# A transformer stack on one core: each background weight-sum transfer gets a panel of its own, and lent slots join the ring at its end

## The reference

```
h = concat(meta, x)                                             # 528 x 1024
h = LN(a1 * h + even_mixer(h));   h = LN(a1 * h + relu(h @ w1)^2 @ w2)   # layer 0, d_ff 4096
h = LN(a1 * h + retention(h));    h = LN(a1 * h + relu(h @ w1)^2 @ w2)   # layer 1
h = h[16:]                                                      # 512 x 1024
h = LN(a2 * h + 0.5 * swiglu1(h));  h = LN(a2 * h + token_mixers(h))     # d_ff 2816
h = LN(a2 * h + cross_attention(h, mem));  out = LN(a2 * h + 0.5 * swiglu2(h))
```

## Time and profile before

| | |
|---|---|
| time, median of 3 runs | 2704.35 us (2703.06 to 2708.93) |
| profiled execution | 2705.15 us, span 2703.2 us, mean granted PE clock 0.992 |
| PE, PEld busy | 2633.5 us, 2347.4 us |
| DVE, ACT, POOL busy | 1455.0, 1120.3, 345.0 us |
| DMA moved | 342.61 MB, of it 79.70 MB by POOL's queue |
| stretches of the span | even mixer to about 305 us, layer 0 chunks 0 to 3 about 335, 421, 510, 598 to 680, retention to 1115, layer 1 chunks from 1185, 1252, 1337, 1422 to 1500, SwiGLU 1 to 1880, mixers to 2165, cross attention to 2300, SwiGLU 2 to the end |

### The profile page before, as it was taken

One profiled execution on the slowest core, in us unless ns is written; L12 is line 12 of the kernel. 1 busy time (PEld: TensorE's weight loads), 2 busy tenths in 40 slices (PEclk: granted clock), 3 DMA queues, 4 the chain that ended last, 5 costly groups with the idle time before them and its releaser, 6 DMA issues.

```text
span 2703.2 us, 41070 instructions
## 1 busy us (share of the span) xinstructions
PE 2633.5 (97%) x16968; PEld 2347.4 (87%) x16968; DVE 1455.0 (54%) x2464; ACT 1120.3 (41%) x1833; POOL 345.0 (13%) x414
## 2 busy tenths in 40 slices
PE   8999999999999999999999999999899999999997
PEld 6888999999988888888888988888888897989997
DVE  5664666446543434575556633334666764654655
ACT  4555444334433233353334432322557543433443
POOL 3100310001311000230000410011311130300002
PEclk9999999999999999999999999999999999999998
DMA  9911275335462512256344382252622132233542
GB/s 340 228 51 48 79 285 158 121 114 160 109 149 64 140 63 84 87 188 220 121 142 157 94 238 91 89 147 66 170 86 71 61 104 65 67 105 130 168 141 67
DMA packets 108840, 342.61 MB, mean 127 GB/s; under 512 B 11248, under 2 KB 13680, under 8 KB 108272
## 3 DMA queue, kind: packets, MB, share of 16 engines
q1 hardware_dynamic: 78448, 260.30, 29.3%
q0 software_dynamic: 30208, 79.70, 12.2%
HBM read 337.83 MB, written 81.79 MB: 155 GB/s over the span
## 4 chain that ended last, share of the span: by engine, by line
PE 86%; DVE 4%; ACT 3%; POOL 2%; issue 2%; DMA 2%; SPq 0%; DVEq 0%; POOLq 0%; ACTq 0%
PE ps L693 61%; PE ps L735 14%; PE ps L1040 2%; POOL R L3077 1%; PE ps L1171 1%; PE ps L743 1%; DMA RAW<-in_wf 1%; PE ps L935 1%; PE ps L895 1%; POOL S L3062 1%; PE ps L1026 1%; ACT HT L1445 1%; DVE HT L2186 1%; DVE R L2193 1%; DMA SCR<-in_wfb 1%
## 5 line engine op out<-in xcount | busy, mean ns | idle before, releaser
L2159 DVE TENSOR_TENSOR WL<-RAW,WH 128x1024 fp32r<-128x1024 f32 (+2 forms) x280 | 338.6, 1210 | 249.9 <-ACT WH L1401 248.5
L693 PE MATMUL ps<-HH,LENT 128*128 128x256 f32 (+2 forms) x1848 | 416.1, 321 | 8.8 <-DVE LENT L2159 8.8
L693 PE MATMUL ps<-XH,WH 128*128 128x264 f32 (+2 forms) x1360 | 412.1, 340 | 12.0 <-DVE XL L3036 7.4
L1401 ACT ACTIVATE WH<-RAW 128x1024 fp32r<-128x1024 f32 (+2 forms) x280 | 287.8, 1032 | 279.8 <-PE ps L693 181.8
L693 PE MATMUL ps<-XL,WH 128*128 128x264 f32 (+2 forms) x1360 | 398.7, 331 | 0.0
L693 PE MATMUL ps<-XH,WL 128*128 128x264 f32 (+2 forms) x1360 | 398.0, 330 | 0.0
L2159 DVE TENSOR_TENSOR LENT<-RAW,LENT 128x1024 fp32r<-128x1024 f32 (+2 forms) x220 | 261.2, 1193 | 181.9 <-ACT LENT L1401 180.2
L693 PE MATMUL ps<-XH,LENT 128*128 128x264 f32 (+2 forms) x1392 | 332.6, 328 | 5.3 <-DVE XL L2210 5.1
L693 PEld LDWEIGHTS ps<-HH,LENT 128*128 128x128 f32 x1848 | 302.9, 190 | 36.2 <-DVE LENT L2159 9.9
L1401 ACT ACTIVATE LENT<-RAW 128x1024 fp32r<-128x1024 f32 (+2 forms) x220 | 216.6, 994 | 276.0 <-PE ps L693 169.0
L693 PE MATMUL ps<-HH,WH 128*128 128x512 f32 (+2 forms) x928 | 285.6, 333 | 10.8 <-DVE HL L2252 6.7
(11 more groups left out here) (266 smaller groups left out, 4022.9 us busy)
## 6 DMA issues: line engine op xcount, KB each, us to landing
RAW<-in_wf SPq DMA_DIRECT2D x104, 512.0 KB, 4.3
sum_wf<-in_wf POOLq DMA_DIRECT2D x36, 1024.0 KB, 30.9
RAW<-sum_wf SPq DMA_DIRECT2D x48, 512.0 KB, 3.8
RAW<-in_wr SPq DMA_DIRECT2D x48, 512.0 KB, 3.5
RAW<-in_wg SPq DMA_DIRECT2D x37, 512.0 KB, 3.5
RAW<-in_wu SPq DMA_DIRECT2D x37, 512.0 KB, 4.1
RAW<-in_wd SPq DMA_DIRECT2D x32, 512.0 KB, 3.5
RAW<-in_we SPq DMA_DIRECT2D x24, 512.0 KB, 6.8
```

What stands on the lines that cost most here:

```text
L693: mm = e.matmul(o[:, to:to + m], wt, xt[:, k, c0 + a * m:c0 + (a + 1) * m], start=(n == 0 and j == 0), stop=(n == nk - 1 and j == 2))
L1401: e.activation(slot(u)[0][:, 0:n], raw[:, 0:n], ACT.Copy).then_inc(*S.w_hi(u))
L2159: e.tensor_tensor(lo[:, 0:n], raw[:, 0:n], hi[:, 0:n].bitcast(F32), ALU.subtract).then_inc(*S.w_lo(u))
```

## The change

Two edits. In `slot_plan` the slots of the three panels in `again` are put at the right end of the ring; all other slots that join are put at the left, as before. On POOL the copies and additions are issued one by one, each behind a wait for a panel that PE has finished: the 24 of layer 0 behind plan panels 3 to 26 of the even mixer, the 24 of layer 1 behind the `wf2` panels of chunks 0 to 2 of layer 0, the 16 of the SwiGLU behind those of chunks 0 and 1 of layer 1. The order is all copies, key by key, then all S1, S3, S2 and S4 additions. They leave the retention, the time after `ln11`, after the memory's norm and after `ln1`.

```diff
         if i in comes:
-            ring.extendleft(reversed(comes[i]))
             if i in again:
+                ring.extend(comes[i])
                 had.update({s: (last_pair(again[i]), 7) for s in comes[i]})
+            else:
+                ring.extendleft(reversed(comes[i]))
...
-        def sum_copies(key):
+        def quarters(key):
...
+        def sum_copy(key, m):
+            a, h = {"S1": (1, 1), "S3": (0, 0), "S2": (0, 0), "S4": (0, 1)}[m]
+            e.dma_start(sums_of(key)[SUM_AT[m]], quarters(key)[a, h]).then_inc(*S.sum_copy(key, m))
...
-        def sum_adds(keys, *ms):
-            for m in ms:
+        def sums_beside(panels, keys):
+            for key in keys:
+                for m in ("S1", "S3", "S2", "S4"):
+                    w.wait_ge(*S.panel[final(next(panels))])
+                    sum_copy(key, m)
+            for m in ("S1", "S3", "S2", "S4"):
                 for key in keys:
+                    w.wait_ge(*S.panel[final(next(panels))])
                     sum_add(key, m)
+
+        def downs(layer, chunks):
+            return iter([AT["wf2", 32 * layer + 8 * c + m] for c in chunks for m in range(8)])
...
-        for key in ff_sums[0]:
-            sum_copies(key)
-        sum_adds(ff_sums[0], "S1", "S3", "S2", "S4")
+        sums_beside(iter(range(3, 28)), ff_sums[0])
         down_norm("ln00")
-        for key in ff_sums[1]:
-            sum_copies(key)
+        sums_beside(downs(0, range(3)), ff_sums[1])
         down_norm("ln01")
         for h in range(4):
-            sum_adds(ff_sums[1], *(("S1", "S3"), ("S2",), ("S4",), ())[h])
...
         down_norm("ln10")
-        for key in gu_sums:
-            sum_copies(key)
+        sums_beside(downs(1, range(3)), gu_sums)
         down_norm("ln11")
-        sum_adds(gu_sums, "S1", "S3")
...
-        sum_adds(gu_sums, "S2")
         down_norm("ln1")
-        sum_adds(gu_sums, "S4")
```

More of the change, by code:

```diff
@@ L3099, in down_norm, with sums_of @@
                 layer_norm(ln, half, T // 2, lambda k: R[:, k, c:c + T // 2], dst, {} if half else between)
-        def sum_copies(key):
+        def quarters(key):
             (name, first), n = key, SUM_PAIRS[key]
[L3104 to L3107, removed]
+            return A[name][first:first + 2 * n].rearrange("(q a) p (h k) c -> a h p q (k c)", a=2, h=2)
+        def sums_of(key):
+            return WSUM[key].rearrange("q p s c -> s p q c")
+        def sum_copy(key, m):
+            a, h = {"S1": (1, 1), "S3": (0, 0), "S2": (0, 0), "S4": (0, 1)}[m]
+            e.dma_start(sums_of(key)[SUM_AT[m]], quarters(key)[a, h]).then_inc(*S.sum_copy(key, m))
         def sum_add(key, m):
-            (name, first), n = key, SUM_PAIRS[key]
-            w4 = A[name][first:first + 2 * n].rearrange("(q a) p (h k) c -> a h p q (k c)", a=2, h=2)
-            to = WSUM[key].rearrange("q p s c -> s p q c")
             w.wait_ge(*S.sum_copy[key, m])
@@ L3118, in sum_add @@
                 w.wait_ge(*S.sum_add[key, "S2"])
-            more = {"S1": w4[1, 0], "S3": w4[1, 0], "S2": to[SUM_AT["S1"]], "S4": to[SUM_AT["S2"]]}[m]
-            e.dma_start(to[SUM_AT[m]], more, accum_op=ALU.add).then_inc(*S.sum_add(key, m))
-        def sum_adds(keys, *ms):
-            for m in ms:
+            more = {"S2": "S1", "S4": "S2"}.get(m)
+            src = sums_of(key)[SUM_AT[more]] if more else quarters(key)[1, 0]
+            e.dma_start(sums_of(key)[SUM_AT[m]], src, accum_op=ALU.add).then_inc(*S.sum_add(key, m))
+        def sums_beside(panels, keys):
[4 more added lines that the diff above has]
+            for m in ("S1", "S3", "S2", "S4"):
                 for key in keys:
+                    w.wait_ge(*S.panel[final(next(panels))])
                     sum_add(key, m)
+        def downs(layer, chunks):
+            return iter([AT["wf2", 32 * layer + 8 * c + m] for c in chunks for m in range(8)])
         ff_sums = [[("wf1", 32 * layer + 8 * c) for c in (1, 2, 3)] for layer in range(2)]
```

## The result

| | before | changed kernel |
|---|---|---|
| median (20 executions each) | 2706.36 us | 2709.63 us (2705.39 to 2713.10) |
| ratio | 1 | 1.0014, 95% interval 1.0007 to 1.0020 |
| second comparison (the run after_again below) | 2705.40 us | 2711.82 us, ratio 1.0023 (1.0012 to 1.0034) |
| profiled execution | 2705.15 us, span 2703.2 | 2713.10 us, span 2711.2 |

The forecast was 2695.5 with a range to 2705. The time is outside, on the other side of no change. One warning on sizes: the profiled execution of the changed kernel lies 3.5 us over its own median, and so does that of the run after_again (2715.26 against 2711.82).

A forecast was written before the change was run, and what follows sets the result against it. PE, busy 97% of the span with 86% of the chain, was taken as the bound, leaving only its waits to save. Gains of 21.7 us less 13 lost gave 8.7 less: 2695.5 us, range 2683 to 2705.

The forecast's parts named there:

- The gains: Waits to vanish: start 3.5, after `ln00` 4.9, after `ln10` 5.2, ring junctions 8.1; together 21.7 us.
- The start: Start of the kernel: PE's waits for the second panel's low part and `wfb` both go, 3.5 us gained.
- `wfb` would land in under 8 us: At the start: a sign that the forecast is right; before, this tiny load took 15.0 us to land.
- Rival 2: After `ln00` and `ln10`: bursts do not make HL late, 10.1 us of gain fail; 2706, no change; chance 0.15.
- the even stage gets them later and thinner than before ... nothing: Even mixer, layer 0's transfers: PE waited for weights only once up to 340 us, so the cost is nothing.
- residual sums that start late because POOL stands in a wait: At `ln00`: two or three sums of about 1 us may start late, five panels to catch up; nothing.
- The price of the pair stages: Pairs behind down panels: a transfer backlog slows loads, 1.75 us per exposed pair beside additions; 13 us lost in all.
- The hidden block behind chunk 2: Layer 1: one late hidden block, counted with 3 x 1.75 in the additions' cost of 6 us (0 to 13).
- the copies of 1.8 MB: Layer 1, copies issued on chunk 0: backlog of up to 2.7 pairs, about 4 us lost (0 to 6).
- Rival 3: Pair stages: three RAW buffers become the bound, 3.3 us a pair over about 12 pairs; 2722; chance 0.08.
- Rival 1: Pair stages: loads share equally with the background, landing in 5.7 us, some 3 us lost; 2685.6; chance 0.27.
- The rule on DMA queues: Engines alternate between queues by packet, so one background transfer slows a load as much as twelve queued; speaks against spreading.

The follow-up runs named there:

- after_again: The changed kernel itself, run and profiled a second time: 2711.82 us, ratio 1.0023 to the kernel before.
- spread_out: Kernel before plus ring edit, layer 0's transfers bunched early, layer 1's and SwiGLU's copies on down panels, their additions as before: 2686.19 us, ratio 0.9930.
- ring_only: Kernel before with the ring edit alone: 2697.70 us against 2705.59, ratio 0.9971.
- gu_only: Kernel before with only the last SwiGLU's 16 transfers spread over the down panels of layer 1: 2712.83 us, ratio 1.0030.
- ff1_only: Kernel before with only layer 1's 24 transfers spread over layer 0's down panels, chunks 0 to 2: 2703.15 us, ratio 0.9996.
- even_early: Changed kernel with layer 0's transfers all issued by panel 20, POOL still waiting for panel 26: 2701.52 us, ratio 0.9987 to the kernel before.

## Why the prediction was wrong, step by step

- **The gains were right.** Forecast 21.7 us. The ledger's rows of gain in the first trace, with 4.8 us for `ln00` (the second row of the ledger holds it beside the loss of 11.0, and spread_out has it alone), sum to 21.1, or 19 to 20 without the 1.1 to 2.5 us of other origin at `ln10`. The start is the shakiest: in ring_only, gu_only and ff1_only, which keep the burst, the same matmul starts at 23.6, 24.0 and 28.5 us instead of 25.5, and in the runs without it at 22.3 to 23.1, so the burst costs anything from about 1 to 6 us there, and the 3.5 that came true was partly luck. That `wfb` would land in under 8 us was wrong (9.4); the wait went all the same. Rival 2, bursts not to blame, falls: without them both waits for HL are gone.
- **The step that failed** is "the even stage gets them later and thinner than before ... nothing". It rested on PE's waits for weights up to 340 us in the trace of before, and on the additions at 62 to 130, beside which PE had no such wait. Both are true and neither bears on the place to which the change moved the last additions. In the heads a plan panel takes some 10 us (the copies behind them were issued at 45.58, 55.07, 62.86 and 76.01), with one load for each. Where the projection ends, SP of before issues ten loads within 20 us, from 279.81 on (two `weo` panels and eight leads), for PE's last 28.68 us before `ln00`, and ACT waits for them 11.5 us. PE lived on panels split in advance, so its own list of waits was empty. The three additions that landed there cost 11 us. I looked up whether PE waited there and not whether the engines that feed it did. With this one term the sum would have been -8.7 + 11 = +2.3. The other way in which the prediction thought of a loss there, residual sums that start late because POOL stands in a wait, it rightly put at nothing: even_early keeps that wait and loses nothing.
- **The price of the pair stages was nearly right.** Forecast 13, measured 15 to 18 over the two traces. The mechanism is the forecast one, to the number: in chunk 2 of layer 1 loads at 6.8 to 6.9 us, ACT waiting for RAW 6.4 us, PE waiting for ACT's evictions, a stage of 46 us (1340.86 to about 1387). In layer 0 only chunk 3 lost in the changed kernel, 2 us; chunk 2, priced for up to two exposed pairs, lost nothing. Two sizes were low. The hidden block behind chunk 2 cost 3.8 us and not under 1, as the load before it is held up too (8.15 us) and the clock is 0.50 from 1393 to 1396, behind the wait of 1.8 us. And the copies of 1.8 MB cost 4.2 to 7.1 us in chunk 1, not 4. That S4 is issued only when S2 has landed, and so inside the pair stage, I had left out. One reading was wrong without a price: the sums of layer 0 are ready not hundreds of us but some 80 us before SP loads them (transfers done by about 310, first load at 392.36).
- **Rivals.** Rival 3 (RAW as the bound at 3.3 us a pair) didn't come about: a pair of chunk 2 lost 5.1 / 4 = 1.3 us. Rival 1 (loads at 5.7 us) neither. The slower outcome had a mechanism that none of them named, so the range ended at 2705.
- **The rule on DMA queues.** The Trainium skill (DMA: Bandwidth & Descriptors, Queues, rings and completion order) has each engine take turns between its queues. The projection's loads took 8.2 us beside a single addition and 8.8 beside three in a row: here the trace agrees that it hardly matters to a load how many are queued behind the one in flight. It was the rule that spoke against the change, and I used it only for its milder reading and not at the stage without slack. That reading, an equal share with loads at 5.7 us (an estimate of mine, not the skill's), is not what was measured: the loads took 6.8 to 8.8 us.
- **The sum again.** -8.7, with 11 for the projection, 2 to 5 more for the pair stages and 2 less gain, is +6 to +9. The ledgers of the two profiled executions sum to +8.1 and +5.1, and their spans differ by +8.0 and +10.1. The medians say +3.3 and +6.4; both profiled executions lay 3.5 us over theirs, and why stays open.

## What to carry to other kernels

Before a background transfer is moved, look at the stage that will receive it, and there at the waits of the engines that feed PE, not at PE's alone. A stage in which PE waits for nothing can still have nothing to spare; here each us of background engine time beside such a stage made it about 0.6 us longer. Spread transfers by what the stage has left (two additions of 1.8 MB in a chunk, three panels apart, were free; eight, one each panel, were not), end them ahead of a stretch that is bound by its loads, and mind that an addition which needs an earlier sum is issued when that has landed, not where it stands.

## What the runs showed of the hardware that was not expected

- A DMA that adds in HBM took nearly twice the engine time of one that copies: 17.4 us for 3.15 MB (5.5 us a MB) and 6.2 for 1.05 MB, against 9.3 us for 3.15 MB of copies (3.0 us a MB). The three additions of 1 MB beside the projection landed after a median of 18.7 us, one alone after 10.6.
- The clock fell behind some waits of PE and not behind others: 0.50 at 305 to 310, with 8 us of idle time; 0.68 and 0.64 at 1275 to 1285 behind a wait of 3.0 us in chunk 1 of layer 1 in one execution of the changed kernel, and 1.00 over that stage in another (longest wait 1.6 us); 0.50 at 1393 to 1396 behind one of 1.8 us.
